# Exponentials of the sample weights ahead of and between two window copies, value transposes two steps behind

## What is computed

```python
h = rms_norm(x, g_pre) @ w_in          # q,k,v,z_A (512 each), HGRN2 q,f,i,z_B (512 each), two gates (1024 each)
# branch A, stick-breaking attention, 8 heads x 64
z = q @ k.T / 8
log_fail = where(mask, log_sigmoid(-z), 0)
after = cumsum(log_fail, reverse=True) - log_fail
o_sb = where(mask, exp(log_sigmoid(z) + after), 0) @ v
# branch B, HGRN2, 4 heads, state 128 x 128, in blocks
o_hg, S_new = hgrn2_chunkwise(q, log(lb + (1 - lb) * sigmoid(f)), i, s0)
u_a = (o_sb * silu(z_A)) @ w_branch_a
u_b = (rms_norm(o_hg) * silu(z_B)) @ w_branch_b
merged = sigmoid(gate_a + b_a) * u_a + sigmoid(gate_b + b_b) * u_b
y = x + rms_norm(merged @ w_out, g_post)
```

## Time and profile before

| | |
|---|---|
| median of three runs | 1127.31 us (1126.78 to 1127.88) |
| the profiled execution | 1126.27 us, of which 1124.5 us span from the first to the last instruction |
| busy PE, DVE, ACT, POOL | 95%, 58%, 51%, 14% of the span |
| mean granted clock of PE | 0.991 of full speed |

### The profile page before, as it was taken

One profiled execution on the slowest core, in us unless ns is written; L12 is line 12 of the kernel. 1 busy time (PEld: TensorE's weight loads), 2 busy tenths in 40 slices (PEclk: granted clock), 3 DMA queues, 4 the chain that ended last, 5 costly groups with the idle time before them and its releaser, 6 DMA issues.

```text
span 1124.5 us, 16695 instructions
## 1 busy us (share of the span) xinstructions
PE 1067.8 (95%) x6302; PEld 984.4 (88%) x6302; DVE 648.3 (58%) x1139; ACT 573.2 (51%) x1263; POOL 153.1 (14%) x148
## 2 busy tenths in 40 slices
PE   3999899999899999899999899999999999999995
PEld 2898778998778998778998778999999999999994
DVE  6856697377797377797287797245423212353117
ACT  4447884367784367884367885546022232252222
POOL 2211102012102011102011102000201100111210
PEclk9999999999999999999999999999999999999998
DMA  6014022115021124021124021125111111111144
GB/s 248 13 65 133 20 82 70 40 50 167 20 94 57 41 74 143 20 94 57 41 87 130 20 94 57 41 70 215 39 38 50 45 38 38 43 52 38 38 188 168
DMA packets 41455, 84.86 MB, mean 75 GB/s; under 512 B 2080, under 2 KB 22176, under 8 KB 41248
## 3 DMA queue, kind: packets, MB, share of 16 engines
q1 hardware_dynamic: 40800, 81.43, 21.7%
q10 hardware_dynamic: 576, 2.36, 0.6%
HBM read 67.27 MB, written 16.52 MB: 75 GB/s over the span
## 4 chain that ended last, share of the span: by engine, by line
PE 75%; DVE 10%; ACT 10%; issue 3%; DMA 1%; SPq 0%; ACTq 0%; DVEq 0%
PE bank L629 51%; PE bank L919 9%; DVE E L1482 3%; PE bank L711 2%; ACT E L1133 2%; ACT SPH L1145 2%; PE bank L741 2%; ACT E L1128 2%; DVE E L1486 1%; DVE xw L1454 1%; PE bank L697 1%; ACT RT L1150 1%; PE bank L639 1%; PE bank L816 1%; PE bank L861 1%
## 5 line engine op out<-in xcount | busy, mean ns | idle before, releaser
L629 PE MATMUL bank<-xl,wh 128*128 128x384 f32 x1344 | 458.1, 341 | 6.8 <-DVE xl L1450 6.8
L629 PE MATMUL bank<-xh,wh 128*128 128x384 f32 x1344 | 456.4, 340 | 5.6 <-ACT xh L1100 3.7
L629 PE MATMUL bank<-xh,wl 128*128 128x384 f32 x1344 | 458.3, 341 | 0.0
L629 PEld LDWEIGHTS bank<-xh,wh 128*128 128x128 f32 x1344 | 254.1, 189 | 13.8 <-issue 11.9
L629 PEld LDWEIGHTS bank<-xl,wh 128*128 128x128 f32 x1344 | 253.9, 189 | 11.7 <-DVE xl L1450 8.3
L629 PEld LDWEIGHTS bank<-xh,wl 128*128 128x128 f32 x1344 | 254.3, 189 | 4.9 <-issue 2.3
L1044 ACT ACTIVATE slot<-bank,ngate 128x384 f32<-128x384 f32 x48 | 27.7, 577 | 184.6 <-PE bank L629 182.0
L1275 DVE CAST wh<-wr 128x1024 fp32r<-128x1024 f32 x64 | 43.7, 682 | 102.7 <-PE bank L629 100.1
L1277 DVE TENSOR_TENSOR wl<-wr,wh 128x1024 fp32r<-128x1024 f32 x64 | 95.8, 1497 | 2.2
L1482 DVE SCALAR_TENSOR_TENSOR E<-E,bank 128x512 f32<-128x512 f32 (+3 forms) x96 | 52.9, 551 | 48.5 <-ACT E L1133 48.3
L1145 ACT ACTIVATE SPH<-E 128x512 fp32r<-128x512 f32 (+2 forms) x80 | 45.4, 567 | 54.5 <-DVE E L1486 35.3
(11 more groups left out here) (214 smaller groups left out, 1609.4 us busy)
## 6 DMA issues: line engine op xcount, KB each, us to landing
wr<-wch SPq DMA_DIRECT2D x64, 512.0 KB, 3.6
KTc<-ckT SPq DMA_DIRECT2D x4, 2048.0 KB, 8.6
Vc<-cv SPq DMA_DIRECT2D x4, 2048.0 KB, 8.1
xw<-xT SPq DMA_DIRECT2D x6, 768.0 KB, 10.1
graw<-gated SPq DMA_DIRECT2D x8, 576.0 KB, 7.8
xres<-xT SPq DMA_DIRECT2D x1, 4608.0 KB, 15.2
yT<-yb SPq DMA_DIRECT2D x6, 576.0 KB, 3.0
okT<-kT ACTq DMA_DIRECT2D x4, 576.0 KB, 3.0
```

Of the source, the lines that this page charges most:

```text
L629: i = nc.tensor.matmul(CH[n % 2][:, 0:WIN], weights[:, k, :], rows[:, k, w * WIN:(w + 1) * WIN], start=(m == 0), stop=(m == 23))
```

## The change

On ACT, the exponentials of the sample weights move from step 1 into step 0: group 0's ahead of the copy of window 0, group 1's between the copies of windows 0 and 1. This holds for the gate windows of the last pair as well. On PE and DVE, the transposes of the recurrence's input windows, and DVE's copies of them, move from one step behind a window's end to two.

```diff
@@ tensor, first loop
-                    for w12 in late:
+                    for w12 in ended(B_PIECES[n - 2]) if n >= 2 else ():
                         turn_recurrence(p, w12)
-                    late = ended(B_PIECES[n])
-                for w12 in late:
+                for w12 in ended(B_PIECES[-2]) + ended(B_PIECES[-1]):
                     turn_recurrence(p, w12)
@@ scalar, second loop
+                def window_aside(w12):
+                    if p + 1 < PAIRS:
+                        window_attention(p + 1, w12)
+                    else:
+                        window_gate(w12 // 6, w12 // 3 % 2, w12 % 3)
+
                         nc.scalar.activation(EQ[:, :], lf[:, :], ACT.Exp).then_inc(s_EX, 1)
-                    if m == 1:
+                        done = ended(A_PIECES[0])
                         for g in range(2):
                             act.wait_ge(s_cs, 2 * p + g + 1)
                             nc.scalar.activation(Es[:, g, :], CUs[:, g, :], ACT.Exp).then_inc(s_as, 1)
+                            for w12 in (done[:1], done[1:])[g]:
+                                window_aside(w12)
+                    if m == 1:
                         for g in range(2):
                             act.wait_ge(s_ast, 3 * p + g + 1)
...
-                    for w12 in ended(A_PIECES[m]):
-                        if p + 1 < PAIRS:
-                            window_attention(p + 1, w12)
-                        else:
-                            window_gate(w12 // 6, w12 // 3 % 2, w12 % 3)
+                    for w12 in ended(A_PIECES[m]) if m else ():
+                        window_aside(w12)
@@ vector, first loop
-                    for w12 in late:
+                    for w12 in ended(B_PIECES[n - 2]) if n >= 2 else ():
                         turn_recurrence(p, w12)
-                    late = ended(B_PIECES[n])
-                    for w12 in late:
+                    for w12 in ended(B_PIECES[n]):
                         window_recurrence(p, w12)
-                for w12 in late:
+                for w12 in ended(B_PIECES[-2]) + ended(B_PIECES[-1]):
                     turn_recurrence(p, w12)
```

## The result

The changed kernel takes 1114.87 us (median of 4, 1114.50 to 1114.93) against 1127.32 for the one before: ratio 0.9889, interval 0.9872 to 0.9906, 12.4 us. Its profiled execution took 1114.50 with a span of 1112.7, 11.8 less than before.

The account below looks back on a forecast made before the run. TensorE's waits were taken to bound the second loops, VectorE and ScalarE the first. Gains 10.2 + 1.2 + 0.75 = 12.1 us off 1126.27 gave 1114.1, stated as 1114.5; forecast 1111.3 to 1117 (0.70), range 1111.3 to 1120 (0.85).

Parts of the forecast that it names:

- The exponentials, 10.2 us: Second (A) loops: TensorE no longer waits for the sample weights' masking; 1.9 us in pairs 0 to 2, 4.5 in pair 3.
- The masking near 182 and 184: Pair 0's second loop: VectorE's two maskings of the sample weights were to come near 182 and 184 us.
- the time to spare: Pair 0's second loop: second masking done at 184.4, TensorE ready at 186.0, so 1.6 us to spare.
- Rival 3: Second loops: GpSimd's two products hold VectorE's masking, so the exponentials bring nothing; 1124.3 us, chance 0.06.
- the slowing by half: Against rival 3: four short VectorE instructions beside GpSimd, slowed by half, cost under 1 us of the 1.6 spare.
- The transposes, 0.3 us a pair: First (B) loops: TensorE's waits mostly move, VectorE's loop gains only 0.3 us a pair, 1.2 in four.
- Pair 2's clock, 0.75: Pair 2's first loop: without the 2.36 us wait, the lower-clock loss goes; 0.75 us, bounds 0 and 0.76.
- 1.6 of the last pair's: Pair 3's second loop: the 1.6 us put to a lower-clock stretch, counted within the exponentials' gain.
- The median: Whole kernel: median of runs shown 1.0 us above the profiled execution, so 1114.1 was stated as 1114.5.
- Rivals 1: Whole kernel: only idle time counts, 7.4 us; clock drops stay or move, first loops give nothing; 1118.9 us, chance 0.15.
- 2 (1105): First loops: TensorE is the bound, so the transposes' 10.3 us of waits count in full; 1105 us, chance 0.05.
- rival 4: First loops: waits become two pauses a pair, the clock falls after all eight; slower, 1127 to 1133 us, chance 0.04.

## Why the prediction was right, and where it wasn't

The forecast was 1114.5, the measurement 1114.87; the sum against the profiled execution 12.1, measured 11.8. By its steps:

- **The exponentials, 10.2 us:** 9.90, by 1.81, 1.81, 1.87 and 4.41 against 1.9 three times and 4.5. The starts were the better ruler than the list's idle time (1.6). All of it lies in the second loops, where it was forecast; 1.6 of the 4.41 is the clock (22.20 against 20.62 in the run with the transposes only).
- **The masking near 182 and 184: wrong, and covered by the time to spare.** Rival 3 described what happens: DVE's masking is held until GpSimd's product ends. Its dismissal failed in one step: the scan beside GpSimd that took 1.49 us as ever was read as not being held. It had started at 180.49, 0.05 us before GpSimd's product at 180.54; whoever comes second waits, and there it was GpSimd: from the scan's end at 181.98 its product took 2.47 us more, as it took 2.48 behind the scan in the changed kernel and 2.52 behind the cast that ended at 182.95 in the run that placed it later. The rows held two signs: the masking at 186.01 took 0.44 us and ended 0.15 us after GpSimd's second product (184.41 + 1.89 = 186.30), and the weight split's 2.04 us stand against 1.23 for the same instruction without GpSimd. The rule of the Trainium skill (GPSIMD Engine Reference, section "Key points") that the two contend for SBUF where a DVE instruction has two inputs there holds for the masking: its 0.3 us became 2.71, far more than the slowing by half that the prediction allowed for. It cost 0.2 us a pair instead of the whole gain, because the hold ended with one instruction and PE had time to spare, 1.92 us to the first transposes and four transposes more to the second group: the second masking ended at 186.18, about when PE's first four transposes did. So the number held by the spare time, and not by the reason given against rival 3; that is luck. By these numbers a product 1 us longer would have cost about 1 us a pair more; that wasn't tried.
- **The transposes, 0.3 us a pair:** 0.22 in pair 0 without the start-up, then 0.22, 0.95 (with the clock) and 0.21. The reason is shown: PE's waits turned up again at the scores and at L711, and taking DVE's split off L711's way brought 1.1 us a pair. The copy's cost at its new place shows too: 0.45 us from 163.02 to the split at 163.47.
- **Pair 2's clock, 0.75, and 1.6 of the last pair's:** gone as forecast, but less sure than the sum had it. These 2.3 us are of the kind that another execution of the kernel before has elsewhere, or doesn't have.
- **The median:** I added 0.4 us to the sum made against the profiled execution; it came out 0.37 above its own profiled one. The reason given, a median 1.0 above the profiled execution, would have made it 1115.1; that 0.4 fits is luck.

Rivals 1 (drops stay, 1118.9) and 2 (1105) are out by the times and by the lengths of the loops; rival 4's eight pauses a run are there, 1.4 and 0.8 us long, and no drop follows them in the changed kernel's profile.

## What to carry to other kernels

An engine that copies in program order can hold a result that another engine waits for, though its input lies ready: look for a wait whose releaser was itself waiting for the waiting engine, and move the short instruction ahead. A wait taken from an engine that isn't the stage's bound only moves; find the next meeting point of the two engines, and what delays the bound just before it (here a weight split) is the next change. When work is moved into VectorE's idle time, see what GpSimd does in that time, and compare only instructions that started after GpSimd's.

## What the runs showed of the hardware

A DVE instruction with two inputs in SBUF that was issued while a GpSimd product ran was held until that product ended, and finished 0.14 (masking), 1.08 (weight split) and 1.22 us (key product) after it: masking 2.71 instead of 0.3 us, weight split 3.57 instead of 1.23, key product 3.05 instead of 1.35 us. If DVE's instruction was first, GpSimd's took longer: 3.92 us beside the scan and 2.96 beside the cast, in both cases 2.5 us from the end of DVE's. DVE's log weights, one of whose inputs is in PSUM, were not held: 0.68 us at 184.20 beside GpSimd's product at 184.10.

A lower granted clock followed the same pause of TensorE in some executions and not in others: 4 of 12 waits of some 2.36 us, 2 of 3 pairs of waits of 1.3 and 1.2 us, 2 of 10 waits of 1.6 to 2.1 us.
